# Expert stage of a transformer block: all experts in 128 blocks on TensorE in place of one gather per selected expert

## The reference

```python
def block(hb):
    q = (hb @ w_pq).reshape(TOK_BLOCK, PEER_HEADS, 2, PEER_DHALF)
    s = jnp.einsum('thpd,hpnd->thpn', q, sub_keys)
    s1, i1 = lax.top_k(s[:, :, 0], 16)
    s2, i2 = lax.top_k(s[:, :, 1], 16)
    cand_s = (s1[..., :, None] + s2[..., None, :]).reshape(128, 8, 256)
    cand_i = (i1[..., :, None] * 128 + i2[..., None, :]).reshape(128, 8, 256)
    top_s, pos = lax.top_k(cand_s, 16)
    idx = jnp.take_along_axis(cand_i, pos, axis=-1)
    gate = jax.nn.softmax(top_s, axis=-1)
    act = jax.nn.gelu(jnp.einsum('thkd,td->thk', expert_u[idx], hb), approximate=False)
    return jnp.einsum('thk,thkd->td', gate * act, expert_v[idx])
```

## Time and profile before

| | |
|---|---|
| median of 3 runs | 2872.12 us (2870.63 to 2872.88) |
| profiled execution | 2872.11 us, span 2870.1 us, mean granted clock 0.967 |
| PE busy | 2405.3 us (84%) |
| DVE busy | 1538.4 us (54%) |
| ACT busy | 706.7 us (25%) |
| POOL busy | 525.6 us (18%) |
| moved by DMA | 658.42 MB, of which 536.90 MB by the gathers |

### The profile page before, as it was taken

The page is one execution under the profiler, slowest core; times in us unless marked ns, Lnnn a source line. Parts: engine busy times, 40 slices in busy tenths (PEclk is TensorE's granted clock), DMA queues, the critical chain, the costliest instruction groups (busy, mean ns, idle before and its releaser), DMA issues.

```text
span 2870.1 us, 26493 instructions
## 1 busy us (share of the span) xinstructions
PE 2405.3 (84%) x9420; PEld 1131.4 (39%) x9420; DVE 1538.4 (54%) x3256; ACT 706.7 (25%) x2067; POOL 525.6 (18%) x516
## 2 busy tenths in 40 slices
PE   5889688799877777777777777788899898999998
PEld 3455268664443222222222222222354343444443
DVE  3555477647336775767566665554439454333204
ACT  1122231110223334333443334433300101111000
POOL 0000000000233344434343444333200000000000
PEclk9989889799999999999999999999999999999999
DMA  3301431211799999999999999999711212212110
GB/s 129 110 4 56 176 119 69 84 50 59 253 335 372 422 421 421 421 421 421 421 418 418 413 419 416 419 422 416 301 59 66 110 51 88 83 64 88 59 74 29
DMA packets 127875, 658.42 MB, mean 229 GB/s; under 512 B 9472, under 2 KB 12160, under 8 KB 61952
## 3 DMA queue, kind: packets, MB, share of 16 engines
q0 software_dynamic: 73728, 536.90, 45.7%
q1 hardware_dynamic: 54016, 119.84, 11.6%
HBM read 654.60 MB, written 2.10 MB: 229 GB/s over the span
## 4 chain that ended last, share of the span: by engine, by line
PE 49%; DMA 30%; DVE 9%; issue 6%; ACT 4%; PEld 1%; POOL 0%; PEldq 0%; SPq 0%; DVEq 0%; ACTq 0%; POOLq 0%
DMA AR<-in_uv,C 29%; PE PA L506 21%; PE PD L506 8%; PE PD L836 7%; PE PA L816 3%; PE PD L906 1%; PE PA L906 1%; ACT C L1153 1%; PE PD L663 1%; PE PD L499 1%; DVE AR L1781 1%; ACT SC L1149 1%; PE PA L721 1%; PE PA L854 1%; PE PA L663 1%
## 5 line engine op out<-in xcount | busy, mean ns | idle before, releaser
L836 PE MATMUL PD<-AR,C 128*128 128x512 f32 x2048 | 1006.8, 618 | 288.0 <-ACT C L1153 287.0
L1781 DVE CUSTOM_DVE_ANT_0 AR<-AR,HN 128x1024 f32<-128x1024 f32 x512 | 626.1, 1224 | 533.1 <-DMA AR<-in_uv,C 530.3
L1924 POOL DMA_INDIRECT AR<-in_uv,C x512 | 525.4, 1026 | 1527.7 <-PE PD L836 780.9
L836 PEld LDWEIGHTS PD<-AR,C 128*128 128x128 f32 x2048 | 352.5, 190 | 923.6 <-ACT C L1153 650.2
L506 PE MATMUL PA<-AR,WR 128*128 128x512 f32 (+1 forms) x720 | 313.0, 603 | 4.7 <-ACT AR L1043 3.2
L1147 ACT ACTIVATE SC<-SC 128x1 f32<-128x1 f32 x512 | 103.8, 203 | 708.2 <-DVE SC L1781 707.8
L506 PE MATMUL PA<-HT,WR 128*128 128x512 f32 (+1 forms) x608 | 246.6, 565 | 0.0
L1153 ACT ACTIVATE C<-C,SC 128x128 f32<-128x128 f32 x512 | 205.5, 401 | 16.8
L506 PEld LDWEIGHTS PA<-AR,WR 128*128 128x128 f32 (+1 forms) x720 | 138.2, 193 | 179.2 <-issue 176.3
L506 PEld LDWEIGHTS PA<-HT,WR 128*128 128x128 f32 x608 | 111.3, 193 | 127.7 <-issue 127.7
L1149 ACT ACTIVATE SC<-SC,C 128x1 f32<-128x1 f32 x512 | 150.8, 294 | 16.6
(11 more groups left out here) (366 smaller groups left out, 2194.4 us busy)
## 6 DMA issues: line engine op xcount, KB each, us to landing
WR<-in_w_ada SPq DMA_DIRECT2D x12, 2048.0 KB, 10.4
WR<-in_w_in SPq DMA_DIRECT2D x11, 2048.0 KB, 7.9
WR<-in_w_up SPq DMA_DIRECT2D x11, 2048.0 KB, 7.9
WR<-in_w_down SPq DMA_DIRECT2D x5, 2048.0 KB, 7.9
AR<-in_uv,C POOLq DMA_INDIRECT x512, 15.3
AR<-in_w_pq SPq DMA_DIRECT2D x3, 2048.0 KB, 12.9
WR<-in_w_o SPq DMA_DIRECT2D x2, 2048.0 KB, 12.5
WR<-in_w_pq SPq DMA_DIRECT2D x2, 2048.0 KB, 7.9
```

The source lines that it names most:

```text
L836: ins = nc.tensor.matmul(acc[half], DG[:, j, :], UV[:, j, D + 512 * half:D + 512 * half + 512], start=(k == 0), stop=(k == NSEL - 1))
L1781: ttr(UV[:, j, 0:D], UV[:, j, 0:D], HN[:, t, :], 1.0, 0.0, ALU.mult, ALU.add, DOT[:, j:j + 1]).then_inc(s["dots"], 1)
L1924: nc.gpsimd.indirect_dma_start(UV[:, ring_slot(turn), :], None, uv, bass.IndirectOffsetOnAxis(ap=IDX[:, t % 2, i:i + 1], axis=0),).then_in ...
```

## The change

In the expert stage there are no gathers any more; the whole POOL program is gone. The 16384 experts are taken in 128 blocks of 128 rows. The work has two passes.

First pass, for each block b: SP has loaded u (in pairs of blocks, 1 MB), PE turns the block with 8 transpositions, ACT copies the result, and PE multiplies it with the normed tokens of all four tiles (`HT`, 8 products of 512 columns). ACT takes gelu of the result and writes it to DRAM (`spill`, 256 KB per block). Beside this the gates are made into a dense matrix: for each tile the two indices and the gates are turned (rank on the partitions, token on the columns), and DVE makes for each token a one-hot matrix of the first index scaled with the gate, and a one-hot matrix of the second index. One product of 128 columns per token gives the token's gates over all 128 x 128 experts. It is done three groups of four tokens per block; a tile's 8 MB matrix goes to DRAM (`gspill`) when it is complete.

Second pass, for each block: v, gelu results and gates are loaded, DVE multiplies the last two, and PE multiplies with v: 4 tiles x 2 halves of 512 columns, summed over all blocks in all eight PSUM banks. The last 8 blocks are done tile after tile.

All queries and scores come ahead of the first pass. Select has 31 steps and runs for one tile after the other. Elsewhere: the norm of the RWKV keys is made on 32 columns per tile set and spread by PE instead of on 4 x 512 columns; the exponentials and products ahead of the inverses have another order; KT and AT are turned behind the first products of the inverses; two of the twelve `w_ada` pieces move into the chain.

```diff
-JOBS ("kn", 0, 4), ("tok", 4, 8), ("inv", 8, 0), ("invz", 24, 48), ("chain", 13, 28) ...
+JOBS ("kn", 0, 5), ("tok", 0, 4), ("inv", 8, 4), ("tok2", 4, 4), ("invz", 24, 44), ("chain", 17, 28) ...
+BLOCKS = 128
+TURNED, LAST = 3, 8
+TI_AT, ROWS_IT = (0, 32, 64, 96), 114
+GROUPS, G_PER = 32, 3
+def groups_at(b):
+    t = max(i for i in range(NT) if TI_AT[i] <= b)
+    first = G_PER * (b - TI_AT[t] - 1)
+    return t, range(max(first, 0), min(max(first + G_PER, 0), GROUPS))
...
@@ SP @@
+            def columns():
+                sp.wait_ge(s["a_full"], FIRST_A["s"] + 12)
+                for pr in range(BLOCKS // 2):
+                    if pr >= TURNED:
+                        sp.wait_ge(s["a_full"], T_JOB[2 * (pr - TURNED) + 1] + 2)
+                    sp.dma_start(UIN[pr % TURNED].rearrange("p (b n) -> p b n", b=2),
+                                 rows_of(2 * pr, 2, 0)).then_inc(u_in[pr % TURNED], 16)
+            def sums(first, last):
+                for gq in range(first, last):
+                    for pr in (2 * gq, 2 * gq + 1):
+                        if pr >= 4:
+                            sp.wait_ge(s["v_used"], 2 * (pr - 4) + 2)
+                        sp.dma_start(VIN[pr % 4], rows_of(2 * pr, 2, 1)).then_inc(v_in[pr % 4], 16)
+                        if pr % 2 == 0:
+                            if gq >= 2:
+                                sp.wait_ge(s["v_used"], 4 * (gq - 2) + 4)
+                            ... (one load of SIN from spill, four of GIN from gspill, for 4 blocks)
@@ PE, RWKV part @@
-            for m in range(4):
-                pe.wait_ge(s["kx_sq"], m + 1)
-                product("d", [(cc("heads"), E1[:, m, :])])
+            pe.wait_ge(s["kx_sq"], 4)
+            ... (16 products of 2 columns into one bank)
+            modulation(1, 3)
+            pe.wait_ge(s["kr"], 1)
+            ... (32 products of 128 columns, 64 rows of output each, into four banks)
-            modulation(6, 12)
+            modulation(5, 10)
+                if c < 2:
+                    modulation_rows(10 + c)
@@ PE, expert stage @@
+            turn_rows(0)
+            for b in range(BLOCKS):
+                if b + 1 < BLOCKS:
+                    turn_rows(b + 1)
+                if b in TI_AT:
+                    t = TI_AT.index(b)
+                    pe.wait_ge(s["gates"], t + 1)
+                    transposes("a", [SS[t][:, 0:NSEL], SS[t][:, NSEL:2 * NSEL], GATE[:, t % 2, :]])
+                t, due = groups_at(b)
+                for q in due:
+                    pe.wait_ge(s["oh"], 5 * (GROUPS * t + q + 1))
+                    oh = OH[q % 4]
+                    bk = bank("a")
+                    for i in range(4):
+                        ins = nc.tensor.matmul(bk[:, P * i:P * i + P], oh[:, 512 + P * i:640 + P * i],
+                                               oh[:, P * i:P * i + P], start=True, stop=True)
+                    full("a", ins)
+                ...
+                pe.wait_ge(s["a_free"], T_JOB[b] + 2)
+                product("a", [(UT[b % 2][:, k, :], HT[:, k, :]) for k in range(KD)])
+            for b in range(BLOCKS - LAST):
+                for t in (2, 3, 0, 1):
+                    ins = weighted(b, t)
+                ins.then_inc(s["v_used"], 1)
+            for t in range(NT):
+                for b in range(BLOCKS - LAST, BLOCKS):
+                    weighted(b, t)
+                if t == 2:
+                    turn_block("xn3", 0, "aa")
+            for t in (1, 2):
+                turn_block("xn3", t, "aa")
@@ ACT @@
+                tell(nc.scalar.copy(gst[:, 4 * q:4 * q + 4, :], bk.rearrange("p (n i) -> p n i", n=4)), "a_free")
+                bk = take()
+                if b >= 4:
+                    act.wait_ge(sw[b % 4], 16 * (b // 4))
+                tell(A(GO[b % 4], bk, ACT.Gelu), "a_free")
@@ DVE @@
-            for m in range(4):
-                dve.wait_ge(s["rstd"], n["var"] - 3 + m)
-                link(nc.vector.reciprocal(E2[:, m, :], E2[:, m, :]))
-                link(tt(KK[:, m, :], KK[:, m, :], E2[:, m, :], ALU.mult))
+            link(nc.vector.reciprocal(rsum, rsum), "kr")
+            def one_hots(t):
+                ti = TI[t]
+                dve.wait_ge(s["a_free"], TI_JOB[t] + 1)
+                for q in range(GROUPS):
+                    ... (waits until the group four back is used)
+                    for i in range(4):
+                        tell(ts(oh[:, P * i:P * i + P], cc("iota"), ti[:, 0, k:k + 1], ti[:, 2, k:k + 1],
+                                ALU.is_equal, ALU.mult), "oh")
+                    tell(tt(oh[:, 512:1024] ..., ALU.is_equal), "oh")
+            gates(0)
+            one_hots(0)
+            for t in range(1, NT):
+                for step in range(STEPS):
+                    select(t, step)
+                gates(t)
+                one_hots(t)
+            for b in range(BLOCKS):
+                ...
+                tell(tt(z, z, GIN[gq % 2][:, :, b % 4, :], ALU.mult), "gated")
@@ POOL @@
-            for t in range(NT):
-                for i in range(NSEL):
-                    nc.gpsimd.indirect_dma_start(UV[:, ring_slot(turn), :], None, uv, ...)
```

More of the change, by code:

```diff
@@ L625, in _ @@
                 product("a", [(lw[64:128, P * m:P * m + P], LT[64:128, 0, :])])
+            pe.wait_ge(s["kx_sq"], 4)
+            b = bank("d")
+            for t in range(NT):
+                for m in range(4):
+                    o = 8 * t + 2 * m
+                    ins = nc.tensor.matmul(b[:, o:o + 2], E1[:, m, P * t:P * t + P], cc("head2"),
+                                           start=True, stop=True)
+            full("d", ins)
             for t in range(NT):
@@ L1031, in modulation @@
                 for i in range(first, last):
-                    tell(nc.scalar.copy(ADAROW[i % 2], take()), "a_free")
-                    if i > 0:
+                    tell(nc.scalar.copy(ADAROW[i], take()), "a_free")
+                    if 0 < i < 10:
                         modulation_columns(i - 1)
@@ L1064, in _ @@
             tell(A(EQ[:, :, :], SG[:, :, :], ACT.Exp, scale=-KAPPA), "rexp")
-            act.wait_ge(s["rexp"], n["rexp"])
-            modulation(6, 12)
-            modulation_columns(11)
-            for t in range(NT):
-                tell(nc.scalar.copy(KTOK[:, t, :], take()), "a_free")
+            tell(A(E1[:, :, :], CS[:, :, :], ACT.Exp, scale=-KAPPA), "rexp")
+            modulation(5, 10)
+            modulation_columns(9)
             for q in range(4):
@@ L1073, in _ @@
                 tell(nc.scalar.copy(UR64[:, q, :], take()[0:64, :]), "a_free")
+            act.wait_ge(s["rexp"], n["rexp"])
+            for t in range(NT):
+                tell(nc.scalar.copy(KTOK[:, t, :], take()), "a_free")
             for lev in range(1, LEVELS):
@@ L1116, in scores @@
                 tell(nc.scalar.copy(SS[t][:, 512 * g4:512 * g4 + 512], take()), "a_free")
-            for j in range(16 - PQ_IN_PEER):
+            for j in range(16):
                 query(j)
+            for t in range(1, NT):
+                for g4 in range(4):
+                    scores(t, g4)
             def gate_exp(t):
@@ new lines, in turned_rows, with spilled @@
+            def turned_rows(b):
+                for i in range(2):
+                    bk = take()
+                    if b >= 2:
+                        act.wait_ge(s["a_full"], U_JOB[b - 2] + 1)
+                    tell(nc.scalar.copy(UT[b % 2][:, 4 * i:4 * i + 4, :], bk.rearrange("p (k n) -> p k n", k=4)),
+                         "a_free")
+            def spilled(b):
+                act.wait_ge(s["a_free"], U_JOB[b] + 1)
+                act.dma_start(spill[:, S * b:S * b + S], GO[b % 4]).then_inc(sw[b % 4], 16)
@@ L1414, in _ @@
             tell(dve.nop(), "rkk")
+            for m in range(4):
+                b = take()
+                link(tt(KK[:, m, :], KK[:, m, :], b, ALU.mult), "d_free")
             b = take()
@@ L1515, in _ @@
                 link(tt(blocks(XP[:, q, :]), blocks(XP[:, q, :]), mask64(IDENT2), ALU.add), "xp")
+            for t in range(NT):
+                tell(nc.vector.tensor_copy(BTOK[:, t, :], take()), "d_free")
             for lev in range(1, LEVELS - 1):
```

378 lines of the change are left out of this document (197 added, 181 removed).

## The result

The changed kernel takes **3574.2 us** (median of 4 runs, 3570.1 to 3577.8), the kernel before 2872.5 us (4 runs, 2870.6 to 2872.9): a ratio of 1.245 (95% interval 1.244 to 1.247), 702 us slower. The forecast was 3563 us, 691 slower, with 3520 to 3650 as its range.

What follows compares the result with a forecast made beforehand. The kernel before was taken as bound by gathered bytes, the changed one by PE's work in series: 713 us more in the expert stage, 22 less in the RWKV part, 2872 + 691 = 3563 us, range 3520 to 3650.

Steps and rivals of the forecast that it cites:

- PE takes the place of the gathers, all in series: Expert stage: transfers traded for a second set of 1024 products, turning and gates on PE; 2106.5 us against 1393.4.
- Queries and scores: Ahead of the first pass: queries 86 us, scores 11, copies waited for 1; 98 us together.
- First u: Behind the scores: PE waits for a whole 1 MB transfer, plus copies of the first turned block; 9.5 us (5 to 16).
- First pass: On PE: products 877 us, transpositions 112, gates 117, turned indices and products with ones 5; sum 1111.
- Second pass and end: Second pass 878 us on PE, then 4 us for the last loads and 6 for scaled copies before the second block.
- Cover of the other engines: Both passes: ACT, DVE and transfers fit beside PE; gate writes taken as nothing, upper end 10 us per tile.
- Behind the stage: From the second block on: taken as nearly the same in both kernels, nothing added.
- the RWKV part: Ahead of the queries: 31 us off, 3 and 2 x 3 given back; net 22 us less, between 0 and 44.
- a falling clock in the first pass: Rival: at a granted clock of 0.89 the first pass's 1111 us become 1248, total 3700; chance 4%.
- The second-pass reads at their worst landing: Rival: second-pass loads become the bound, four blocks 37.5 us instead of 27.4, 323 us more, 3886; chance 4%.
- A product at 0.43 us when PE is alone: Rival: dense products run at half the measured time, 878 us less, 2685, faster than before; chance 1%.
- Transpositions that don't overlap: Rival: each of the first pass's 1024 transpositions takes 0.27 us, 164 us more, 3727; chance 3%.

Runs made afterwards that it cites:

- e2: The changed kernel with only one of each four transpositions of u, copies and waits kept: 3491.5 us.
- e3: The changed kernel with only one of each four products that make the dense gates, 384 products fewer: 3508.0 us.
- e7: The changed kernel with bfloat16 operands for its new products, and activations and gates kept in DRAM between the passes also in bfloat16: 2490.4 us.
- e8: The kernel before with only the changes of the RWKV part, its expert stage with gathers untouched: 2862.6 us, ratio 0.9965.
- e11: The changed kernel with 8 unused products of 512 columns right ahead of the inverses: 3570.5 us.
- e6: The changed kernel with the operands of its new products rounded to bfloat16, activations and gates kept in DRAM still float32: 2456.9 us.
- e4: The changed kernel without 360 of the 1024 products of the second pass, all transfers kept: 3268.8 us.
- e5: The changed kernel with 7 further unused 512-column products in the modulation stage, ahead of the inverses: 3574.6 us.
- e1: The kernel before with gathers of 4 KB in place of 8 KB rows: 2514.2 us.

## Why the prediction was right, and where it was off

- **PE takes the place of the gathers, all in series.** Right: the stretch was forecast at 2106.5 us and has 2103.3. The forecast of the whole, 3563, adds up with what each part was off: - 3.2 here, + 13.6 in the RWKV part and + 3.4 behind the stage give 3577, and the profiled execution had 3576.8.
- *Queries and scores*: 671.72 to 767.8, 96 us (98 forecast). *First u*: PE waited 6.20 us and began the first product at 777.74, 9.9 us behind the scores (9.5). That this fits so well is partly luck: the first 16 transpositions took 3.4 us, at a granted clock of 0.50 up to 777, which the forecast didn't have.
- *First pass*: 1109.2 us from the first product (777.74) to the second pass (1111). Its three prices are shown by e2 (0.108 for a transposition), by e3's timeline (0.223 for a gate product) and by the distances between blocks: 16 records in 6.87 us, 0.859 a product.
- *Second pass and end*: 883.5 us with the last loads (878 + 4), one wait of 1.42 us near the end where 4 us were forecast; then 4.6 us of scaled copies (6).
- *Cover of the other engines*: right. No selection and no gate held PE up, and the 2 MB gate writes (15.3 us to land) didn't either. ACT's gate copies took 1.06 us, not the 0.59 that I took for a copy with a stride; they stayed hidden in float32 and held the first pass up as soon as PE was faster and they were written as bfloat16 (e7, 2.86 us each).
- *Behind the stage*: taken as equal, 3.4 us more. The second block's first products took 23.84 us behind the idle 4.56, at a granted clock of 0.87, and 20.88 us in the kernel before at 1.00. The forecast had the idle time, but not the lower clock behind it, 3.0 us.
- **The step that was mis-sized: the RWKV part, -22 forecast and -8.4 measured** (-8.6 in e8's times). The forecast was 31 off ahead of the inverses, 3 back for the copies moved behind their first products and 6 for two pieces in the chain. Measured: the inverses start at 383.55 against 406.30, 22.75 off. Then 12.0 back by the next level (23.7 us against 11.7), where 3 were forecast for the moved transpositions; 9.3 of them are the granted clock, by e11. From there to the queries 2.3 came back, not 6. So 13.6 us missing = 8.3 ahead of the inverses + 9.0 in them - 3.7 behind them. For the 8.3, the stretch from the last products that both kernels share up to the inverses, of the kernel before and then after:

```profile
316.28:406.30 90.02, 57.95 (x370) 32.40 (x369) 54.27 (x63) 24.78 (x43) 0.00 (x0) 0.77 0.65 233
```

```profile
314.80:383.55 68.75, 55.89 (x377) 34.29 (x377) 37.41 (x54) 18.67 (x32) 0.00 (x0) 0.75 0.80 291
```

PE's idle time fell from 32.1 to 12.9 us, 19.2 of the 22.4 forecast (13.4 + 9); what is left are waits for w_ada (6.1 us, 7.2 before), whose transfers the lower bound named, and for ACT (6.5 us, 3.7 before). PE's busy time fell by 2.1 us only, where the 8 of the pieces were forecast. One reason shows: the 16 new products of two columns for the sums take 5.3 us (314.80 to 320.09), and the forecast had nothing for them. Against these two stands 1.5 us that the kernel after was early already (and the forecast's own terms add up to 30.4, not 31). The prediction looked for a falling clock in the first pass, where it stayed at 1.00, and not in the RWKV part, where the change takes the 128-column transpositions away from in front of the 64-column products.
- *Rivals.* The second-pass reads at their worst landing: out, 1 MB of activations landed in 4.8 us. That their rows lie 256 KB apart in DRAM didn't slow them visibly: in e6, where transfers set the pace, all reads together ran at 406 GB/s. A product at 0.43 us when PE is alone: out, e4. Transpositions that don't overlap: out in time, e2. The record of each says 275 ns, the figure that the Trainium skill ("TensorE: Matmul & The Clock Gate", Part 4: PE-mode transpose) gives for one in a kernel, in bfloat16; in a row of eight between products each took 0.109 us of PE's time. On the other half of that rule, that they don't count as activity, the running first pass is silent, since 8 long products stand between 8 of them and the clock stayed at 1.00. Its beginning speaks against it: behind 6.20 us without work PE did nothing but transpositions from 773.99 to 777.74, and in them the granted clock rose from 0.50 to 1.00.

Not settled: which part of what stands ahead of the inverses decides their clock. 16 records of 512 columns right ahead kept it at 1.00 (e11), two of them with 16 one-column records behind didn't (e5). In the kernel before, 32 transpositions stood there and it was 1.00 as well, but no version was tried that moves them back alone.

## What to carry to other kernels

Before a transfer-bound stage is replaced by dense work, count the list of the engine that will bound it as if it were alone: here PE had 1.73 us of a 2.49-us turn already, and the dense form gave it 1095 us more against 399 that it had to spare. Count it by the distance between records in a packed row, since the busy time of scattered ones is larger. Here the dense form paid off only with cheaper products (bfloat16, 0.22 us against 0.86), and then ACT's strided copies and the spilled bytes, free until that moment, are the next bound and must be priced too. A forecast must also price what a change adds in the place where it takes something away (the products for the sums in the RWKV part). When work is moved, look at what it leaves next to each other on TensorE, not only at the waits.

## What the runs showed of the hardware

- A copy by ACT from PSUM, 128x512, with scattered writes: 1.06 to 1.10 us for float32 at 512 bytes, 2.86 us for bfloat16 at 256 bytes; 0.61 us with the stride on the reading side and runs of four elements on the writing side; 0.59 us without stride.
- With 4 KB rows instead of 8 KB a gather's span on POOL, which is a rough measure, grew from 1.03 to 1.29 us, though half the bytes moved; the stage then ran at 300 GB/s, with PE as its bound, instead of 420.
- Four records of a float32 product that stand alone count 1.98 us of busy time, four in a packed row take 1.73 us (e1).
- With 8 products of 512 columns right ahead, the first part of the inverses (products of 64 columns, then transpositions) had a granted clock of 1.00; with 16 one-column records there, 0.57 from 383.55 to 407.29, though PE was as busy.
- Behind an idle time of 6.20 us the granted clock rose from 0.50 to 1.00 while PE did only transpositions (773.99 to 777.74).
- A float32 transposition of 128x128 has a record of 275 ns and takes 0.109 us of PE's time in a row of eight between products.
